# Ranking over 128 sums, picks of eight heads at a time on VectorE, and the one-hot gates of two pairs of tokens spread in one group

## The chip, the cores and the metric

One core of a Trainium2 chip runs the kernel. The metric is the device time of one execution in microseconds (us), and less is better. Engines are named as the profile names them: PE (TensorE; PEld is its weight loads), DVE (VectorE), ACT (ScalarE), POOL (GpSimd) and SP (SyncE, which issues the weight DMAs).

## The reference, cut to what matters

An encoder block over 256 tokens of width 2048, all float32: norm, projections, two kinds of attention, gates, an output projection, and then the part that this case is about, a product-key expert layer.

```python
q = (t @ w_pq).reshape(n_tok, 8, 2, 128)
sc = einsum('thcd,hckd->thck', q, sub_keys)          # (256, 8 heads, 2 halves, 128 keys)
top_s, top_i = lax.top_k(sc, 16)
cand_s = top_s[:, :, 0, :, None] + top_s[:, :, 1, None, :]      # 16 x 16 sums per head
cand_i = top_i[:, :, 0, :, None] * 128 + top_i[:, :, 1, None, :]
best_s, best_j = lax.top_k(cand_s, 16)
expert_idx = take_along_axis(cand_i, best_j)         # 8 heads x 16 experts of 16384
gate = softmax(best_s)
out[t] = sum over its 128 experts e of  gate * gelu(u[e] . t) * v[e]
```

## The kernel before, in words

**Chunks and bodies.** Every weight matrix goes through the core in chunks of 128 x 1024 floats (512 KB). Per chunk SP loads `raw` (four buffers), ACT rounds it into `hi` (L620, four buffers), DVE makes the rest `lo = raw - hi` (`lo_of`, L1000, two buffers), and PE multiplies `hi` by both halves of the activations (eight wide matmuls, "highs") and `lo` by the first half (eight narrow ones, "lows"). An even chunk goes highs, lows; an odd one lows, highs. So the order on PE is H0 L0 L1 H1 H2 L2 L3 H3. Four chunks are a body; slot `s` of body `it` is one chunk. On DVE slot `s` begins with `lo_of(s + 1)` and then holds other work, so a `lo` waits for what the slot before put on DVE's queue, and for the chunk two earlier to be done with its buffer. The order of work is written out by hand; each engine's queue is strictly in order.

**The expert layer.** 224 of the 256 tokens are computed densely: stage `u` (256 chunks, 64 bodies) makes gelu(u . t) for all 16384 experts, row block by row block of 128, into `act`; stage `down` (256 chunks, 64 bodies in two halves of 32) multiplies `act` by v. The last 32 tokens are computed from gathered rows: 64 gathers of `u_rows` by POOL (L574, buffers `rows0`, `rows1`), each followed by a dot product on DVE (`dot_of`, L1426), then 64 gathers of `w_down` rows, each added by DVE (`rows_at`, L1539 and L1542). `gather("u_rows", n)` waits for `dot_done >= n - 1`, `gather("w_down", n)` for `row_added >= n - 1`.

**Ranking.** In bodies 1 to 16 of stage `u` DVE ranks one head of one token half each (`best`): the 16 x 16 sums `cand` (L1338), the best 8 (L1341), replaced (L1344), indexed (L1348), the next 8 (L1351, L1354), then the two digits of the place (L1357 to L1361) and a one-hot comparison `pick` (L1364). POOL multiplies it by the key numbers (L563), and DVE sums it in the next body (`reduce_picks`, L1372). Body UR = 17 divides the softmax, PE turns gates and numbers after it, and body 18 copies them for the next stage.

**Spreading the gates.** From body U0 = 19 for 28 bodies, one pair of tokens per chunk: DVE makes `one_i` (`ones_of`, L1458, one buffer), POOL makes `one_j`, times the gate (L594, two instructions a pair, two buffers of a pair), PE multiplies them in full float32 ahead of the chunk (L1848, four recorded passes a pair), ACT copies the blocks still to come into `act` (L898), and DVE multiplies the blocks that are there (`gated_of`, L1467). DVE also multiplies `act` by each block's gelu (L1474). There is one dot per body at slot 3 (it follows the pair's work), and POOL's loop puts `gather("u_rows", k + 3)` ahead of pair 4k + 2. Bodies 47 to 63 hold no spreading and two dots each.

**Down.** The rows of each half are added at chunk 8 + 3.5 m of the half (`adds_of`). After each half PE's sums are kept as tiles. In the second half ACT squares eight tiles in slot 3 of bodies 33 and 34 (L959), and POOL, after `gather("w_down", 33)`, waits for both squares, folds them (three instructions of L607) and only then issues gather 34.

Body numbers of `down` go on to count from 0 at its first chunk.

Of the kernel before, what the change touches and what calls it, by code (L numbers as in the profile page):

```python
# [15 lines left out]
P = 128  # L16
# [72 lines left out]
UR = TT * PH + 1  # L89
# [33 lines left out]
DIVIDED = PH + 2  # L123
INDEXED = DIVIDED + 2

def dots_of(it, s):

    if it < UG:
        return (it - UR,) if s == 3 and it >= UR else ()
    return (UG - UR + 2 * (it - UG) + s // 2,) if s % 2 else ()  # L130


def adds_of(c):

    return tuple(m for m in range(PICKS) if 8 + m * 7 // 2 == c)
# [90 lines left out]
def build(nc, A, out):  # L226
    with ExitStack() as ctx:
# [47 lines left out]
        one_i = small("one_i", [P, 2, P])  # L275
        one_j = [small(f"one_j{i}", [P, 2, P]) for i in range(2)]
# [44 lines left out]
        cand = at("cand", ARENA + 104 * KB, [P, TOPK * TOPK])  # L321
        cand_b = at("cand_b", ARENA + 105 * KB, [P, TOPK * TOPK])
        pick = at("pick", ARENA + 106 * KB, [P, 2, TOPK, TOPK])
        pick_b = at("pick_b", ARENA + 96 * KB, [P, 2, TOPK, TOPK])
        best_s = at("best_s", ARENA + 108 * KB, [P, TOPK])
        best_j = at("best_j", ARENA + 108 * KB + 64, [P, TOPK], U32)
        half_u = at("half_u", ARENA + 108 * KB + 128, [P, 2, TOPK], U32)
        half_f = at("half_f", ARENA + 108 * KB + 256, [P, 2, TOPK])
        soft_sum = at("soft_sum", ARENA + 108 * KB + 448, [P, TT * PH])
# [69 lines left out]
        picked, picked_row = sem("picked"), sem("picked_row")  # L399
# [121 lines left out]
        def _(pool):  # L521
# [35 lines left out]
            kept = top_i[:].rearrange("p t h c k -> p (t h) c k")  # L557
            pool.wait_ge(top_kept, HC + 2)
            for first, row in ((0, PH), (PH, -PH)):
                with pool.Fori(first, first + PH) as it:  # L560
                    pool.wait_ge(picked, it + 2)
                    r = kept[:, bass.ds(it + row, 1), :, :].rearrange("p a c k -> p (a c) k").unsqueeze(2).to_broadcast([P, 2, TOPK, TOPK])
                    nc.gpsimd.tensor_tensor(pick_b[:], pick[:], r, ALU.mult).then_inc(picked_row, 1)  # L563

# [49 lines left out]
        def _(a):  # L614
# [244 lines left out]
            with a.Fori(1, DIVIDED - 1) as it:  # L859
                body("u", it, gelu_kept)  # L860
            body("u", DIVIDED - 1, gelu_and_exp)
            with a.Fori(DIVIDED, INDEXED) as it:
                body("u", it, gelu_kept)
            body("u", INDEXED, gelu_and_index)
            with a.Fori(INDEXED + 1, UR) as it:
                body("u", it, gelu_kept)

# [7 lines left out]
            body("u", UR, lambda it, s: (gelu_kept(it, s), exp_of(0, 2 * PH) if s == 1 else None))  # L875
# [9 lines left out]
            def gelu_split(j, e):  # L885
# [3 lines left out]
                if t < TD:  # L889
                    nc.scalar.activation(act[:, j, t:TD], upper[e][:, t:TD], ACT.Gelu)  # L890
                nc.scalar.activation(upper[e][:, 0:t], upper[e][:, 0:t], ACT.Gelu).then_inc(act_ready, 1)

            def keep_gates(it, s):
# [71 lines left out]
            down(0, 0, after=gelu_w)  # L965
            with a.Fori(1, HALF - 1) as it:
# [25 lines left out]
        def _(v):  # L992
# [331 lines left out]
            halves = top_s[:].rearrange("p t h c k -> p (t h) c k")  # L1324
            cut, cut2 = [P, TOPK, TOPK], [P, 2, TOPK, TOPK]

            def of_head(t, it):
                return t[:].rearrange("p t (h k) -> p (t h) k", k=TOPK)[:, bass.ds(it, 1), :].rearrange("p a k -> p (a k)")

            def best(body_it, s, row_of, before=None):  # L1330

                keep_u(body_it, s)
                it = row_of(body_it)
                if s == 0:
                    v.wait_ge(picked, body_it)
                    a = flat(halves[:, bass.ds(it, 1), 0, :]).unsqueeze(2).to_broadcast(cut)
                    b = flat(halves[:, bass.ds(it, 1), 1, :]).unsqueeze(1).to_broadcast(cut)
                    did(nc.vector.tensor_tensor(cand[:].rearrange("p (a b) -> p a b", a=TOPK), a, b, ALU.add))  # L1338
                    wait()
                    settle()  # L1340
                    did(nc.vector.max(best_s[:, 0:8], cand[:]))  # L1341
                    wait()
                    settle()
                    did(nc.vector.match_replace(cand_b[:], best_s[:, 0:8], cand[:], LOWEST))  # L1344
                if s == 1:
                    if before:
                        reduce_picks(body_it - 1, before(body_it - 1))
                    did(nc.vector.max_index(best_j[:, 0:8], best_s[:, 0:8], cand[:]))  # L1348
                    wait()
                    settle()  # L1350
                    did(nc.vector.max(best_s[:, 8:16], cand_b[:]))  # L1351
                    wait()
                    settle()
                    did(nc.vector.max_index(best_j[:, 8:16], best_s[:, 8:16], cand_b[:]))  # L1354
                if s == 2:
                    wait()
                    did(nc.vector.tensor_scalar(half_u[:, 0, :], best_j[:], 4, None, ALU.logical_shift_right))  # L1357
                    did(nc.vector.tensor_scalar(half_u[:, 1, :], best_j[:], 15, None, ALU.bitwise_and))
                    did(nc.vector.tensor_scalar(of_head(found_g, it), best_s[:], best_s[:, 0:1], None, ALU.subtract))
                    wait()  # L1360
                    did(nc.vector.tensor_copy(half_f[:], half_u[:]))  # L1361
                    wait()

                    nc.vector.tensor_tensor(pick[:], half_f[:].unsqueeze(3).to_broadcast(cut2),  # L1364
                                            iota16[:].unsqueeze(1).unsqueeze(1).to_broadcast(cut2), ALU.is_equal
                                            ).then_inc(picked, 1)

            def reduce_picks(done, row):

                v.wait_ge(picked_row, done)  # L1370
                ij = found_ij[:].rearrange("p c t (h k) -> p c (t h) k", k=TOPK)[:, :, bass.ds(row, 1), :]
                nc.vector.tensor_reduce(ij.rearrange("p c a k -> p c (a k)"), pick_b[:], AX.X, ALU.add).then_inc(best_ready, 1)  # L1372

            def row_1(body_it):
                return body_it + (PH - 1)

            def row_0(body_it):
                return body_it - (PH + 1)
            v.sem_inc(picked, 1)
# [4 lines left out]
            def divided(tt, step):  # L1384
                g = found_g[:, tt, :].rearrange("p (h k) -> p h k", k=TOPK)
                total = soft_sum[:, tt * PH:(tt + 1) * PH]
                if step == 0:
                    v.wait_ge(soft_ready, TT - tt)
                    did(nc.vector.tensor_reduce(total, g, AX.X, ALU.add))
                    wait()  # L1390
                    did(nc.vector.reciprocal(total, total))
                if step == 1:
                    wait()
                    return nc.vector.tensor_tensor(g, g, total.unsqueeze(2).to_broadcast([P, PH, TOPK]), ALU.mult)

            def best_and_divide(it, s):
                best(it, s, row_0, row_0)
                if s == 0:
                    divided(1, 0)
                if s == 1:  # L1400
                    did(divided(1, 1))
                if s == 2:
# [625 lines left out]
```

## Time and profile before

| | |
|---|---|
| time of the three runs | 2187.15 us median (2185.96 to 2187.82) |
| the profiled execution | 2187.54 us, its span 2185.8 us |
| busy share of the span | PE 97%, DVE 74%, ACT 51%, POOL 25% |
| mean granted PE clock | 0.991 |
| stage `u`, ranking bodies 1 to 16 | 794.0 to 975.9 us |
| first spreading body (19) | 996.7 to 1014.5 us |
| the other 27 spreading bodies | 1014.5 to 1341.7 us |
| bodies 48 to 63, nothing added | 1351.8 to 1512.7 us |

A body of plain chunks issues 64 matmuls, a spreading body 80. Positions are us from the span's start. In a timeline a row is a run of like instructions of one engine; in brackets behind it is the idle time of the engine ahead of it and what ended it. Consecutive DVE instructions overlap by some 0.08 us in their records.

### The profile page before, as it was taken

The page shows a single profiled execution, that of the slowest core. Times are in us where ns is not written, and L with a number is a line of the kernel's source. Part 1 is how long each engine was busy: PE and PEld are TensorE (multiplying, and loading weights), DVE is VectorE, ACT ScalarE, POOL GpSimd, SP SyncE. Part 2 cuts the span into 40 slices and gives each one's busy share as a digit, 9 for nine tenths or more (in the row PEclk, how much of TensorE's full clock was granted, in tenths as well). Part 3 has the DMA queues.
Part 4 walks back from the last instruction along what each step waited for, and adds up shares of the span by engine and source line. Part 5 has one row for each costly group of instructions (what it writes and reads, how often), then busy time and mean ns, then how long its engine had stood idle before and what let it go on. Part 6 is the DMA issues. An engine that isn't in the chain of part 4 may idle for free.

```text
span 2185.8 us, 41303 instructions
## 1 busy us (share of the span) xinstructions
PE 2128.4 (97%) x13474; PEld 1983.1 (91%) x13474; DVE 1609.3 (74%) x2656; ACT 1120.9 (51%) x1867; POOL 545.7 (25%) x403
## 2 busy tenths in 40 slices
PE   7999999999999999999999999999999999999997
PEld 6888888889988998888999999999999999899996
DVE  6555566667777889996777888887777776777776
ACT  5444455446454554555555555555555555555454
POOL 0000000000002001127999996332111110211110
PEclk9999999999999999999999999999999999999999
DMA  5655544445555555556666666898877776677773
GB/s 213 243 186 191 182 165 154 146 152 202 183 186 210 171 177 183 183 202 214 217 214 220 212 216 254 308 317 301 287 278 267 268 261 220 234 274 270 265 268 130
DMA packets 134460, 482.17 MB, mean 221 GB/s; under 512 B 15423, under 2 KB 18239, under 8 KB 134007
## 3 DMA queue, kind: packets, MB, share of 16 engines
q1 hardware_dynamic: 115958, 414.27, 54.2%
q0 software_dynamic: 18432, 67.12, 8.4%
q8 instruction: 26, 0.43, 0.1%
q14 instruction: 44, 0.35, 0.0%
HBM read 477.09 MB, written 4.24 MB: 220 GB/s over the span
## 4 chain that ended last, share of the span: by engine, by line
PE 55%; DVE 4%; issue 3%; ACT 1%; POOL 1%; DVEq 0%; ACTq 0%; POOLq 0%
PE ps L1861 19%; PE ps L1600 15%; PE ps L1865 10%; PE ps L1607 8%; PE ps L1848 3%; DVE lo L1000 1%; POOL one_j L594 1%; ACT hi L620 1%; DVE found_ij L1372 0%; DVE best_s L1351 0%; DVE best_j L1348 0%; DVE upper L1006 0%; DVE best_j L1354 0%; DVE x L1588 0%; PE ps L1917 0%
## 5 line engine op out<-in xcount | busy, mean ns | idle before, releaser
L1000 DVE TENSOR_TENSOR lo<-raw,hi 128x1024 fp32r<-128x1024 f32 x760 | 949.9, 1251 | 484.2 <-PE ps L1600 146.9
L620 ACT CAST hi<-raw 128x1024 fp32r<-128x1024 f32 x760 | 794.7, 1051 | 367.5 <-DMA raw<-w_down 143.0
L1600 PE MATMUL ps<-move_u,hi 128*128 128x448 f32 x2048 | 454.5, 370 | 0.0
L1861 PE MATMUL ps<-act_now,hi 128*128 128x448 f32 x2048 | 442.6, 367 | 0.4 <-issue 0.4
L1861 PEld LDWEIGHTS ps<-act_now,hi 128*128 128x128 f32 x2048 | 377.2, 189 | 26.8 <-issue 0.7
L1600 PEld LDWEIGHTS ps<-move_u,hi 128*128 128x128 f32 x2048 | 374.0, 190 | 24.7
L1600 PE MATMUL ps<-move,hi 128*128 128x512 f32 x1536 | 381.2, 397 | 10.7 <-ACT hi L620 10.0
L1600 PEld LDWEIGHTS ps<-move,hi 128*128 128x128 f32 x1536 | 282.6, 190 | 64.9 <-issue 9.9
L628 ACT COPY upper<-ps 128x224 f32<-128x224 f32 (+1 forms) x224 | 80.0, 357 | 485.6 <-PE ps L1600 485.3
L594 POOL TENSOR_SCALAR one_j<-iota,j_t,gate_t 128x128 f32<-128x128 f32 x224 | 295.7, 1326 | 10.6 <-PE ps L1848 8.9
L1607 PE MATMUL ps<-move_u,lo 128*128 128x224 f32 x2048 | 267.3, 278 | 14.7 <-DVE lo L1000 14.6
L1607 PEld LDWEIGHTS ps<-move_u,lo 128*128 128x128 f32 x2048 | 255.1, 192 | 21.6 <-DVE lo L1000 18.0
L1865 PEld LDWEIGHTS ps<-act_now,lo 128*128 128x128 f32 x2048 | 251.4, 192 | 9.3 <-issue 3.2
L1865 PE MATMUL ps<-act_now,lo 128*128 128x224 f32 x2048 | 252.7, 275 | 4.2 <-DVE lo L1000 4.2
L1607 PEld LDWEIGHTS ps<-move,lo 128*128 128x128 f32 x1536 | 198.7, 193 | 14.4 <-DVE lo L1000 4.2
L574 POOL DMA_INDIRECT rows<-w_down,idx x64 | 93.5, 1462 | 460.6 <-DVE acc L1542 423.1
L1607 PE MATMUL ps<-move,lo 128*128 128x256 f32 x1536 | 202.0, 285 | 5.2 <-DVE lo L1000 4.0
L574 POOL DMA_INDIRECT rows<-u_rows,idx x64 | 90.6, 1416 | 123.8 <-DVE dots L1426 110.8
L1507 DVE TENSOR_TENSOR act_now<-act,act_now 128x224 fp32r<-128x224 f32 x256 | 99.7, 390 | 14.3 <-ACT act_now L913 14.2
L1630 PE MATMUL ps<-move,hi 128*128 128x256 f32 x512 | 99.2, 291 | 3.7 <-DVE lo L1000 3.7
L527 POOL COPY q_now<-qk 128x256 f32 x8 | 4.1, 512 | 370.3 <-DVE qk L1013 213.8
L913 ACT CAST act_now<-act 128x224 fp32r (+1 forms) x256 | 95.3, 373 | 0.0
(194 smaller groups left out, 1710.0 us busy)
## 6 DMA issues: line engine op xcount, KB each, us to landing
raw<-w_u SPq DMA_DIRECT2D x256, 512.0 KB, 3.4
raw<-w_down SPq DMA_DIRECT2D x256, 512.0 KB, 3.5
raw<-w_qk SPq DMA_DIRECT2D x68, 512.0 KB, 3.3
raw<-w_gate SPq DMA_DIRECT2D x64, 512.0 KB, 3.3
raw<-w_out SPq DMA_DIRECT2D x32, 512.0 KB, 3.3
raw<-w_pq SPq DMA_DIRECT2D x32, 512.0 KB, 4.1
raw<-w_v SPq DMA_DIRECT2D x28, 512.0 KB, 3.3
raw<-w_o SPq DMA_DIRECT2D x24, 512.0 KB, 3.3
```

The costliest lines, as they stand in the source:

```text
L574: nc.gpsimd.indirect_dma_start(rows[n % 2][:], None, lines, bass.IndirectOffsetOnAxis(ap=idx[:, n:n + 1], axis=0)).then_inc(row_landed[n % ...
L594: ins = nc.gpsimd.tensor_scalar(one_j[n % 2][:, t % 2, :], iota128[:], j_t[:, t:t + 1], gate_t[:, t:t + 1], ALU.is_equal, ALU.mult)
L620: nc.scalar.copy(hi[slot][:], raw[slot][:]).then_inc(hi_ready, 1)
L628: nc.scalar.copy(upper[e][:, 0:w], ps[e][:, w:2 * w]).then_inc(upper_ready, 1)
L913: nc.scalar.copy(act_now[s % ACTS][:, 0:TD], pick1(act, j)).then_inc(act_hi_ready, 1)
L1000: nc.vector.tensor_tensor(lo[s % LOS][:], raw[s % RAW][:], hi[s % RAW][:].bitcast(F32), ALU.subtract).then_inc(lo_ready, 1)
L1507: nc.vector.tensor_tensor(act_now[s % ACTS][:, TD:2 * TD], pick1(act, j), act_now[s % ACTS][:, 0:TD].bitcast(F32), ALU.subtract).then_inc( ...
L1600: ins = nc.tensor.matmul(ps[bank][:, 0:2 * w], hi[slot][:, col:col + P], m, start=begins, stop=ends)
L1607: ins = nc.tensor.matmul(ps[bank][:, 0:w], lo[lslot][:, col:col + P], m[:, 0:w], start=False, stop=False, skip_group_check=True)
L1630: ins = nc.tensor.matmul(ps[bank][:, 0:T], w[:, col:col + P], x, start=begins, stop=ends)
L1861: return nc.tensor.matmul(ps[d][:, 0:2 * TD], hi[s % RAW][:, d * P:(d + 1) * P], act_now[s % ACTS][:], start=begins, stop=ends)
L1865: return nc.tensor.matmul(ps[d][:, 0:TD], lo[s % LOS][:, d * P:(d + 1) * P], act_now[s % ACTS][:, 0:TD], start=False, stop=False, skip_gro ...
```

## The change

Four things. **(1) Ranking:** of the 256 sums only 128 places are formed, 4 x 16 and 4 x 12 with 16 filled once; the ranking of a head is cut into the four slots, and its scores and places are kept. **(2) Picks:** digits, places and one-hot picks are made for all eight heads of a token half at a time, 1024 elements wide in two parts, all on DVE, by a table of slots (`PICK_AT`); POOL's multiply is gone. UR goes from 17 to 22, so everything behind it, spreading included, begins five bodies later, and bodies 1 to 21 are written out. **(3) Spreading:** pairs 2i and 2i + 1 are spread together, ahead of the even chunks alone, into one bank; `one_i` has two buffers, `one_j` four. **(4) Rows:** ten of the 64 dots move into bodies 0 to 4 of `down`; the adds of the first half come at chunk 28 + 2.75 m, those of the second at chunk 2 + 3.5 m.

```diff
-UR = TT * PH + 1
+UR = TT * PH + 6
 U0 = UR + 2
 J_KEPT = 2 * U0 - 1
...
+TOGETHER = 2
+def spread_at(n):
+    return SPREAD_BANKS[n // TOGETHER % SPREADS], n % TOGETHER * 2 * P
 def pairs_before(j):
-    return min(max(0, 2 * (j - J_KEPT) + 1), PAIRS)
+    return min(max(0, 2 * (j - J_KEPT)), PAIRS)
 def blocks_before(n):
-    return J_KEPT + (n + 1) // 2
+    return J_KEPT + n // 2 + 1
...
-DIVIDED = PH + 2
-INDEXED = DIVIDED + 2
+INDEXED = UR - 2
+PICK_AT = {1: {PH + 1: (0, 1, 2, 3), PH + 2: (4, 5, None, 6), PH + 3: (None, 7, None, 8), PH + 4: (None, None, None, 9),
+               PH + 5: (None, 10, None, 11), PH + 6: (None, None, None, 12), PH + 7: (None, 13, None, 14),
+               PH + 8: (None, None, None, 15), PH + 9: (None, 16, None, 17)},
+           0: {2 * PH + 1: (0, 1, 2, 3), 2 * PH + 2: (4, 5, 6, 7), 2 * PH + 3: (None, 8, 9, 10),
+               2 * PH + 4: (None, 11, 12, 13), 2 * PH + 5: (14, 15, 16, 17)}}
+SOFT_AT = {1: ((PH + 1, 0), (PH + 1, 2), (PH + 3, 0), (PH + 3, 2), (PH + 4, 0)),
+           0: ((2 * PH + 1, 0), (2 * PH + 1, 2), (2 * PH + 3, 0), (2 * PH + 4, 0), (2 * PH + 5, 0))}
+EXP_AT = {1: PH + 2, 0: 2 * PH + 2}
+WEIGHED = (STEPS - (UG - UR) - 2 * (CHUNKS["u"] // BODY - UG) + 1) // 2
 def dots_of(it, s):
     if it < UG:
         return (it - UR,) if s == 3 and it >= UR else ()
-    return (UG - UR + 2 * (it - UG) + s // 2,) if s % 2 else ()
-def adds_of(c):
-    return tuple(m for m in range(PICKS) if 8 + m * 7 // 2 == c)
+    n = UG - UR + 2 * (it - UG) + s // 2
+    return (n,) if s % 2 and n < STEPS else ()
+def adds_of(c, half):
+    first, apart = (2, 7 / 2) if half else ((WEIGHED + 2) * BODY, 11 / 4)
+    return tuple(m for m in range(PICKS) if first + int(m * apart) == c)
...
 # POOL: the multiply by top_i (L563) is gone; the loop over pairs
             for n in range(PAIRS):
                 if n % BODY == 2:
                     gather("u_rows", n // BODY + 3)
-                if n >= 2:
-                    pool.wait_ge(gates_spread, n - 1)
+                if n >= 2 * TOGETHER:
+                    pool.wait_ge(gates_spread, n - 2 * TOGETHER + 1)
                 for t in (2 * n, 2 * n + 1):
-                    ins = nc.gpsimd.tensor_scalar(one_j[n % 2][:, t % 2, :], iota128[:], j_t[:, t:t + 1], gate_t[:, t:t + 1],
+                    ins = nc.gpsimd.tensor_scalar(one_j[n % 4][:, t % 2, :], iota128[:], j_t[:, t:t + 1], gate_t[:, t:t + 1],
                                                   ALU.is_equal, ALU.mult)
...
 # DVE: ranking in four slots
+                if s == 0:
                     wait()
+                    did(nc.vector.tensor_tensor(cand[:, 0:4 * TOPK].rearrange("p (a b) -> p a b", b=TOPK),
+                                                s0[:, 0:4].unsqueeze(2).to_broadcast([P, 4, TOPK]),
+                                                s1.unsqueeze(1).to_broadcast([P, 4, TOPK]), ALU.add))
+                    did(nc.vector.tensor_tensor(cand[:, 4 * TOPK:8 * TOPK].rearrange("p (b a) -> p b a", b=4)[:, :, 4:TOPK],
...
+                keep_u(b, s)
+                wait()
+                if s == 0:
                     did(nc.vector.max(best_s[:, 0:8], cand[:]))
+                if s == 1:
+                    did(nc.vector.match_replace(cand_b[:], best_s[:, 0:8], cand[:], LOWEST))
+                    did(nc.vector.max_index(best_at[:, 0:8], best_s[:, 0:8], cand[:]))
+                if s == 2:
+                    did(nc.vector.max(best_s[:, 8:16], cand_b[:]))
+                if s == 3:
+                    did(nc.vector.max_index(best_at[:, 8:16], best_s[:, 8:16], cand_b[:]))
...
 # DVE: picks 6 to 17 are four times (compare, multiply, reduce) over [P, 4 heads, 16, 16]
+                found = [P, PH // 2 * TOPK, TOPK]
+                if n % 3 == 0:
+                    return did(nc.vector.tensor_tensor(pick[:].rearrange("p h k a -> p (h k) a"),
+                                                       at_ij[:, c, own].unsqueeze(2).to_broadcast(found),
+                                                       iota16[:].unsqueeze(1).to_broadcast(found), ALU.is_equal))
+                if n % 3 == 1:
+                    return did(nc.vector.tensor_tensor(pick[:], pick[:], top_i[:, tt, heads, c, :].unsqueeze(2)
+                                                       .to_broadcast([P, PH // 2, TOPK, TOPK]), ALU.mult))
+                return did(nc.vector.tensor_reduce(found_ij[:, c, tt, own], pick[:].rearrange("p h k a -> p (h k) a"), AX.X, ALU.add))
...
-            def ones_of(it, s):
-                n = it * BODY + s
-                if n:
-                    v.wait_ge(gates_spread, n)
+            def ones_of(n):
+                if n >= TOGETHER:
+                    v.wait_ge(gates_spread, n - TOGETHER + 1)
...
+            def spread_gates(it, s):
+                n = (it - U0) * BODY + s
+                if n + TOGETHER < PAIRS:
+                    ones_of(n + TOGETHER)
                 keep_u(it, s)
+                if n >= TOGETHER:
+                    gated_of(n - TOGETHER)
                 multiply_split(it, s)
                 dots_at(it, s)
...
 # PE: ahead of slots 0 and 2
+                    for m in range(s, s + TOGETHER):
+                        bank, col = spread_at(k * BODY + m)
+                        pe.wait_ge(one_i_ready, n + (m + 1))
+                        pe.wait_ge(one_j_ready, n + (m + 1))
+                        if not (isinstance(it, int) and it < U0 + 2):
+                            pe.wait_ge(gated, n + (m + 1 - 2 * BODY))
+                        for u in range(2):
+                            ins = nc.tensor.matmul(ps[bank][:, col + u * P:col + (u + 1) * P], one_i[m % 2][:, u, :],
+                                                   one_j[m % 4][:, u, :], start=True, stop=True)
+                        ins.then_inc(gates_spread, 1)
...
 # ACT: keep_gates waits for both pairs of its group; exp and the w_s gelu at their new bodies
+                a.wait_ge(gates_spread, n - n % TOGETHER + TOGETHER)
```

## Rows read from the trace of the kernel before

**Rows 1.** Windows: stretch and length, busy us (instructions) by engine, granted PE clock, DMA.

```profile
794.00:996.70 202.70, 188.14 (x1162) 176.06 (x1160) 182.53 (x369) 107.47 (x166) 37.95 (x21) 0.99 0.54 191
996.70:1014.50 17.80, 14.85 (x83) 14.19 (x83) 8.88 (x18) 6.57 (x13) 13.70 (x13) 0.81 0.55 187
1014.50:1341.70 327.20, 324.87 (x2162) 305.61 (x2161) 260.84 (x486) 173.65 (x378) 312.47 (x241) 1.00 0.64 217
1527.00:1820.00 293.00, 293.00 (x1867) 279.84 (x1867) 213.60 (x268) 153.66 (x233) 46.91 (x32) 1.00 0.76 273
1868.10:1884.00 15.90, 13.04 (x65) 12.11 (x65) 10.89 (x11) 5.72 (x9) 6.71 (x5) 0.79 0.55 199
```

**Rows 2.** Groups of DVE's instructions by shape, 600 to 1000 us.

```profile
L1364 DVE TENSOR_TENSOR pick<-half_f,iota 128x512 f32<-128x512 f32 x16 | 11.1, 693 | 0.6
```

**Rows 3.** Timeline of PEld in a middle spreading body, 1086 to 1099 us.

```profile
1086.44 0.61 PEld L1848 LDWEIGHTS ps<-one_j,one_i 128*128 128x128 f32 x4
1089.48 0.53 PEld L1848 LDWEIGHTS ps<-one_j,one_i 128*128 128x128 f32 x4
1089.93 0.97 PEld L1607 LDWEIGHTS ps<-move_u,lo 128*128 128x128 f32 x8
1092.76 0.52 PEld L1848 LDWEIGHTS ps<-one_j,one_i 128*128 128x128 f32 x4 [0.42 <-issue]
```

**Rows 4.** Timeline of DVE and POOL in that body, and of DVE in body 46.

```profile
1083.93 1.23 DVE L1000 TENSOR_TENSOR lo<-raw,hi 128x1024 fp32r<-128x1024 f32 x1 [1.14 <-PE ps L1607]
1085.79 1.22 DVE L1426 CUSTOM_DVE_ANT_0 rows<-rows,h_rows 128x1024 f32<-128x1024 f32 x1
1089.85 1.22 DVE L1000 TENSOR_TENSOR lo<-raw,hi 128x1024 fp32r<-128x1024 f32 x1 [0.80 <-PE ps L1607]
1089.96 1.78 POOL L594 TENSOR_SCALAR one_j<-iota,j_t,gate_t 128x128 f32<-128x128 f32 x1
1092.82 1.23 DVE L1000 TENSOR_TENSOR lo<-raw,hi 128x1024 fp32r<-128x1024 f32 x1 [1.01 <-PE ps L1600]
...
1326.99 1.23 DVE L1000 TENSOR_TENSOR lo<-raw,hi 128x1024 fp32r<-128x1024 f32 x1 [0.64 <-PE ps L1607]
1329.19 1.21 DVE L1426 CUSTOM_DVE_ANT_0 rows<-rows,h_rows 128x1024 f32<-128x1024 f32 x1
```

**Rows 5.** Timelines at two later bodies: a POOL instruction just ahead of a DVE one.

```profile
1250.90 0.80 POOL L594 TENSOR_SCALAR one_j<-iota,j_t,gate_t 128x128 f32<-128x128 f32 x1
1251.05 1.36 DVE L1000 TENSOR_TENSOR lo<-raw,hi 128x1024 fp32r<-128x1024 f32 x1 [0.81 <-PE ps L1600]
...
1263.25 1.84 POOL L594 TENSOR_SCALAR one_j<-iota,j_t,gate_t 128x128 f32<-128x128 f32 x1
1263.36 1.23 DVE L1000 TENSOR_TENSOR lo<-raw,hi 128x1024 fp32r<-128x1024 f32 x1 [0.77 <-PE ps L1600]
```

**Rows 6.** Timeline behind a dot in a body without spreading.

```profile
1385.95 1.23 DVE L1426 CUSTOM_DVE_ANT_0 rows<-rows,h_rows 128x1024 f32<-128x1024 f32 x1
1387.46 1.68 POOL L574 DMA_INDIRECT rows<-u_rows,idx  x1 [3.09 <-DVE dots L1426]
```

**Rows 7.** Timeline and a window at two waits of PE, and the start of spreading.

```profile
905.27 1.15 PE L1607 MATMUL ps<-move_u,lo 128*128 128x224 f32 x8 [1.94 <-DVE lo L1000]
906.70:909.90 3.20, 3.20 (x10) 2.85 (x9) 3.17 (x5) 0.84 (x3) 1.28 (x1) 0.50 0.34 132
996.47 4.58 POOL L594 TENSOR_SCALAR one_j<-iota,j_t,gate_t 128x128 f32<-128x128 f32 x4
```

**Rows 8.** Timeline of the fold in `down`, and gather 34's issue to landing.

```profile
1866.18 6.02 POOL L607 TENSOR_TENSOR sq<-sq 128x1024 f32<-128x1024 f32 x3 [56.72 <-ACT sq L959]
1866.82 3.43 DVE L1542 SCALAR_TENSOR_TENSOR acc<-rows,w_s,acc 128x1024 f32<-128x1024 f32 x1
1873.41 0.72 PEld L1865 LDWEIGHTS ps<-act_now,lo 128*128 128x128 f32 x3 [3.01 <-issue]
...
DMA to landing us min/median/max: 5.5/5.5/5.5
```

More of the change, by code:

```diff
@@ L964, in kept_tiles @@
                         ins.then_inc(x2_scaled, 1)
-            down(0, 0, after=gelu_w)
-            with a.Fori(1, HALF - 1) as it:
+            down(0, 0)
+            with a.Fori(1, WEIGHED) as it:
+                down(it, 0)
+            down(WEIGHED, 0, after=gelu_w)
+            with a.Fori(WEIGHED + 1, HALF - 1) as it:
                 down(it, 0)
@@ L1322, in keep_u, with rank @@
                     sum_of("u", it * 2, 0, upper[0][:, 0:TD], TD)
[L1324 to L1333, printed above, removed]
+            def rank(b, s):
+                tt, h = (1, b - 1) if b <= PH else (0, b - PH - 1)
+                own = slice(h * TOPK, (h + 1) * TOPK)
+                s0, s1 = top_s[:, tt, h, 0, :], top_s[:, tt, h, 1, :]
+                best_s, best_at = found_g[:, tt, own], best_j[:, tt, own]
@@ L1343, in best @@
[L1343 to L1348, printed above, removed]
-                    wait()
[L1350 to L1354, printed above, removed]
@@ new lines, in softmax_of @@
+            def softmax_of(tt, step):
+                g = found_g[:, tt, :].rearrange("p (h k) -> p h k", k=TOPK)
+                total = soft_sum[:, tt, :]
+                over = [P, PH, TOPK]
+                wait()
+                if step == 0:
+                    did(nc.vector.tensor_copy(first_s[:], g[:, :, 0]))
+                if step == 1:
+                    nc.vector.tensor_tensor(g, g, first_s[:].unsqueeze(2).to_broadcast(over), ALU.subtract).then_inc(best_ready, 1)
+                if step == 2:
+                    v.wait_ge(soft_ready, TT - tt)
+                    did(nc.vector.tensor_reduce(total, g, AX.X, ALU.add))
+                if step == 3:
+                    did(nc.vector.reciprocal(total, total))
+                if step == 4:
+                    did(nc.vector.tensor_tensor(g, g, total.unsqueeze(2).to_broadcast(over), ALU.mult))
@@ new lines, in experts_of @@
+            def experts_of(b, s):
+                if b <= 2 * PH:
+                    rank(b, s)
+                else:
+                    keep_u(b, s)
+                for tt in (1, 0):
+                    for step in range(5):
+                        if SOFT_AT[tt][step] == (b, s):
+                            softmax_of(tt, step)
+                    n = PICK_AT[tt].get(b, (None,) * BODY)[s]
+                    if n is not None:
+                        pick_of(tt, n)
+                if (b, s) == PAIR_AT[0]:
+                    wait()
+                    did(nc.vector.scalar_tensor_tensor(out=e_pair[:, 0, :], in0=found_ij[:, 1, 1, :], scalar=float(NK),
+                                                       in1=found_ij[:, 0, 1, :], op0=ALU.mult, op1=ALU.add))
+                if (b, s) == PAIR_AT[1]:
+                    wait()
+                    nc.vector.tensor_scalar(e_pair[:, 1, :], e_pair[:, 0, :], float(NK * NK), None, ALU.add).then_inc(e_ready, 1)
```

221 lines of the change are left out of this document (90 added, 131 removed).

## The prediction

> **What bounds the kernel now.** I read the page first: PE is the busiest engine by far, so in most stages the time is PE's own and only its waits can be won or added. Then windows by stage. Plain chunks cost PE 293.0 us for 1867 matmuls, which is 10.04 us for the 64 of a body, and there it never waits. Against that, the 18 bodies from 794.0 to 996.7 us take 202.7, the first spreading body 17.8 at a granted clock of 0.81, the other 27 spreading bodies 327.2 (12.12 each), and one body of `down` 15.9 at a clock of 0.79 [rows 1]. Everything the change can do lies in those four excesses: 202.7 - 18 x 10.04 = 22.0, then the first spreading body, then the 27, then 15.9 - 10.04 = 5.9. In all of them I then read the timeline, to see which engine PE waits for last.
>
> In a spreading body (positions from its first spread, T = 1086.44) PE spreads a pair at T, at T + 3.04 and at T + 6.32, the last one 0.42 late; without that wait it is at T + 5.90, so an undisturbed body is 2 x 5.90 = 11.80. A pair's passes take 0.45 (1089.48 to 1089.93) [rows 3]. What was late is POOL: in the window of the 27 bodies it is busy 312 of 327 us [rows 1]. It is that slow because of DVE: a `one_j` instruction takes 0.8 us alone, but 1.78 when it starts at 1089.96, just behind a DVE `lo` (1089.85 to 1091.07): it ends 0.67 after the `lo` does [rows 4]. One that starts 0.15 ahead of a `lo` still goes through in 0.80, one that starts 0.11 ahead takes 1.84 [rows 5]. So a POOL instruction that begins inside a `lo`, or under some 0.13 ahead of it, is held to the `lo`'s end and ends 0.65 after it.
>
> **Ranking and picks.** A DVE instruction over 512 elements takes 0.69 [rows 2], one over 1024 takes 1.22 [rows 4], so 0.16 plus 1.04 per 1024: 0.29 for 128, 0.4 for 224. Half a plain body is 5.02. With two `lo` (2.45), one sum (0.4), the two candidate instructions (0.4), one max (0.3) and a replace and an index with their loads (0.7), slots 0 and 1 come to 4.3; before, the same work over 256 elements, the second max and index and POOL's sum stood there, and that was the excess. A pick adds 1.22: 5.5 in bodies 11, 13 and 15, which is 0.5 over each. Slots 2 and 3 with a pick are 4.7 and fit. In bodies 18 to 20 halves with two picks are 5.3 (0.3 over, three times); body 21 has four picks, 10.9 in all, 0.9 over. I add 1.2 for body 1, which still starts behind the last key ranking, 0.5 for each of the two exponentials (their table loads delay ACT's `hi`), and 1.4 for the turns of gates and numbers, which PE now pays without a wait to hide one in. Sum 1.2 + 1.5 + 1.0 + 1.8 + 1.4 = 6.9; no wait for `found_ready` (it is set a body earlier). Gain 22.0 - 6.9 = **-15.1**. If all picks hid it would be -19; if each of the 24 wide picks showed half its 1.22, -2 or so.
>
> **The start of spreading.** POOL's first four `one_j` took 996.47 to 1001.05 [rows 7]. Before, PE needed two of them; the first group needs four, so PE waits 2 x 0.78 longer: **+1.5**. POOL's queue there holds nothing else than gather 3, which was behind them anyway.
>
> **The other 27 bodies.** This is the part that decides. With four buffers POOL may run two groups ahead, but its queue is in order, and gather k + 3 stands ahead of pair 4k + 2. That gather waits for `dot_done >= k + 2`, so for the dot of slot 3 of the body before the one that uses pair 4k + 2. POOL gets to it early, waits there, and then has to make the gather and four instructions (pairs 4k + 2 and 4k + 3) before PE's second group. Before, it had only two to make, and PE could take the last pair one chunk later. Step by step, from T:
>
> - Both pairs are now ahead of the even chunk, so even chunks end 0.44 later, odd ones as before. DVE's `lo` of slots 1 and 3 (before at T + 3.41 and at T - 2.51) move to T + 3.85 and T - 2.07; that of slot 2 stays at T + 6.38, which is 0.5 behind PE's second spread point.
> - The dot begins 1.86 after the slot 3 `lo` (1083.93 to 1085.79) and ends at T + 0.57 [rows 4]. After: T + 1.01. Its distance grows, as `act` fills, to 2.20 in the last spreading body [rows 4], so the end runs from about T + 0.92 to T + 1.35.
> - Behind a dot the next `lo` follows at once, and a gather that waited for the dot starts 0.28 after its end and takes 1.68 [rows 6]. It ends at T + 2.97.
> - First `one_j`: T + 3.01 to 3.79. The second would start at 3.79, only 0.06 ahead of the `lo` at 3.85: held, it ends at 5.07 + 0.65 = 5.72. Third: 6.50. The fourth starts inside the `lo` of T + 6.38 to 7.61 and ends at 8.27. PE starts 0.23 after it, at T + 8.50, which is 2.60 late: a body of **14.40**. In the earliest bodies the second starts 0.15 ahead and passes; then the third is held (5.72), the fourth ends at 6.51, PE is 0.84 late: a body of 12.64. By the drift that should be some four bodies, and 23 are of the long kind.
> - Then PE's clock. Where the matmuls stood 1.94 us idle (905.27), the granted clock is 0.50 from 906.7 to 909.9 [rows 7]; where they waited 3.01, the body lost 5.9, so 2.85 beyond the wait itself [rows 1, 8]. The 2.3 us gap of a long body lies between. I take the lesser, 3.2 us at half speed, 1.6 us: **16.0** a body. Bounds: none (14.4) and 2.85 (17.25).
>
> 4 x 12.64 + 23 x 16.0 = 418.6, against 327.2: **+91.4**.
>
> The Trainium skill bears on the lock. "SBUF — State Buffer", section "Who interferes with whom", says that a DVE instruction with two SBUF inputs contends only with GpSimd's reads, that one side is then fully blocked for the other's whole instruction, and that descriptor generation is inferred not to be touched by such an instruction. By the first half the trace agrees (1.78 against 0.80); by the last, a gather behind a dot would not be stretched by the `lo` beside it and would end sooner, the second instruction would pass, and the sum would be that of rival B, 2199. I go by the measured 1.68.
>
> **Rows of the last 32 tokens.** The dots moved into `down` meet plain bodies whose DVE has room; the same two a body were hidden in bodies 48 to 63, where PE never waited. I cost them and the denser adds (a row every 6.9 us, against 5.5 to land) at nothing, up to 2 if landings run late.
>
> The second half's adds are another matter. Add 2 of that half comes at chunk 2 + 7 = 9, slot 1 of body 34; before it was chunk 15. Its row is gather 34, which POOL issues only behind the fold, and the fold waits for ACT's square in slot 3 of body 34. DVE therefore stands in slot 1 for something that slot 3 starts, and the `lo` for chunk 3 of the body is behind it. Nothing deadlocks, since ACT runs a chunk or two ahead. In time: the fold started at 1866.18 and took 6.02, with a DVE add of 3.43 in its way, which is 1.28 of work; with DVE idle I take 4.1, so 1870.3; the gather 0.3 later, 5.5 to land: 1876.1; add, rest and `lo`, 2.8: 1878.9 [rows 8]. PE would take that `lo` at about 1865.3 (before, it took its lows there without a wait): 13.6 late. The clock goes to half as it did before, 2.85 more. Against the 5.9 that the fold cost before, which falls away: 13.6 + 2.85 - 5.9 = **+10.6**. If the fold is as slow as before, 12.5; if the row lands sooner by 1, 9.6.
>
> **Sum.** Profiled execution 2187.5 (span 2185.8 and 1.7 around it; 0.4 over the median, no more than the runs' spread): 2187.5 - 15.1 + 1.5 + 91.4 + 10.6 = **2276**.
>
> **The rivals.** *A: the long bodies, but the clock stays up.* Against it: both waits above were followed by half clock, the one of 1.94 too; for it: ranking's excess of 1.2 a body was not, and a wait can fall well or badly for the clock. 4 x 12.64 + 23 x 14.40 = 381.8, +54.6: 2239. *B: the second `one_j` passes each time.* It stands 0.06 from the edge, and my positions are good to 0.1 or so; against it is the drift of the dot's end by 0.4. 27 x 12.64 = 341.3, +14.1: 2199. *C: the clock loses more, 2.85 a body.* +120: 2305. *D, the other side: POOL keeps pace.* If the gather found its dot done, deeper buffers would hide all of POOL and the body would be 11.80: 318.6, -8.6, so 2187.5 - 15.1 + 1.5 - 8.6 + 10.6 = 2176. It decides at a last `one_j` by T + 5.67; four of them and the gather from the dot's end need 0.28 + 1.68 + 0.04 + 4 x 0.78 = 5.1 even unheld, so the dot would have to end by T + 0.5, and not be held once. In its favour is only that the two engines' order could settle otherwise than I read it. *E: the row of add 2 does not stop DVE:* 16 less in any case; B with E would be 2182.
>
> **How the numbers follow.** Main case 0.42, A 0.21, B 0.14, C 0.10, D 0.10, something else 0.03. The likeliest gives 2276; its own range is 2262 to 2290, by the number of long bodies (18 to 27) and the ranking's bounds. For 8 in 10 the range reaches from B to C, 2197 to 2305. 0.2% (4.4 us) is about what a measurement of this kernel can tell. Faster by more: D and B with E, 0.12; within: 0.03; slower: 0.85.
>
> **What would show it.** Ranking bodies of 10.04 with little PE idle; `found_ij` on DVE at 1.22 each. In the spreading stage POOL idle ahead of gathers on DVE's dots (none before), gathers of 1.68, `one_j` at 1.8 twice a body, PE waiting on `one_j` ahead of every second chunk alone, and a granted clock near 0.85. In `down`, one wait of DVE for gather 34 of over 12 us. The prediction is wrong in its main term if PE's waits ahead of L1848 are under 1 us, in the clock if they are 2.3 and the clock reads 0.99, and in the last if no `rows` wait shows at body 34.

## The result and the profile after

The changed kernel takes 2226.93 us (median of four runs, 2223.38 to 2231.48), against 2187.49 before: 1.018 times as long, interval 1.016 to 1.020, or 39.4 us slower. The forecast was 88.5 slower. Its profiled run took 2223.38 (span 2221.6), the lowest of the four, so the trace explains 35.8 us of the 39.4. Two of the four runs are 7 to 8 us longer; they have no trace, and what they lost is open.

First the page of after: busy shares, and the chain that ended last.

```profile
PE 2125.2 (96%) x13474; PEld 1982.0 (89%) x13474; DVE 1581.3 (71%) x2612; ACT 1112.0 (50%) x1863; POOL 456.1 (21%) x387
...
PE 83%; POOL 8%; DVE 4%; issue 4%; DMA 1%; ACT 0%; DVEq 0%; SPq 0%; ACTq 0%; POOLq 0%
...
L607 POOL TENSOR_SCALAR one_j<-iota,j_t,gate_t 128x128 f32<-128x128 f32 x224 | 225.4, 1014 | 1.2
```

POOL has less work than before (21% against 25%) and still holds 8% of the chain. That points to something that POOL waits for, and not to the amount of its work. Then the windows of after, for the same stretches as [rows 1]: the 23 ranking bodies, the first spreading body, the other 27, and the slow body of `down`.

```profile
793.70:1027.30 233.60, 232.51 (x1482) 221.30 (x1480) 186.50 (x367) 130.27 (x203) 4.87 (x5) 1.00 0.65 211
1027.30:1045.80 18.50, 14.85 (x83) 13.90 (x83) 8.73 (x16) 6.19 (x13) 12.66 (x13) 0.82 0.53 173
1045.80:1418.30 372.50, 329.87 (x2162) 310.70 (x2161) 262.81 (x485) 167.40 (x379) 261.36 (x240) 0.99 0.54 190
1891.00:1915.50 24.50, 12.54 (x64) 11.65 (x63) 8.99 (x12) 6.00 (x10) 9.28 (x7) 0.72 0.42 146
```

Ranking: 233.6 less 23 plain bodies of 10.04 leaves 2.7, where it was 22.0: -19.3. First spreading body: +0.7. The 27: 372.5 against 327.2, +45.3. Body of `down`: 24.5 against 15.9, +8.6. Together +35.3, and the spans differ by 35.8. The last columns say something else: the 27 bodies ran at a granted clock of 0.99, not near 0.85.

The waits in the window of the 27 bodies:

```profile
POOL rows L587 <- DVE dots L1451: 109.8, 27, 6.4
...
PE ps L1877 <- POOL one_j L607: 39.1, 25, 1.8
```

POOL stands ahead of all 27 gathers, 4.1 us each; PE then waits for `one_j`. One middle body (T = 1096.65), DVE, POOL, PEld and PE:

```profile
1096.45 1.22 DVE L1451 CUSTOM_DVE_ANT_0 rows<-rows,h_rows 128x1024 f32<-128x1024 f32 x1
1097.59 1.22 DVE L1018 TENSOR_TENSOR lo<-raw,hi 128x1024 fp32r<-128x1024 f32 x1
1100.51 1.23 DVE L1018 TENSOR_TENSOR lo<-raw,hi 128x1024 fp32r<-128x1024 f32 x1 [0.77 <-PE ps L1631]
1103.04 1.23 DVE L1018 TENSOR_TENSOR lo<-raw,hi 128x1024 fp32r<-128x1024 f32 x1 [0.58 <-PE ps L1624]
...
1097.95 1.77 POOL L587 DMA_INDIRECT rows<-u_rows,idx  x1 [3.79 <-DVE dots L1451]
1099.75 8.27 POOL L607 TENSOR_SCALAR one_j<-iota,j_t,gate_t 128x128 f32<-128x128 f32 x8
...
1102.64 0.55 PEld L1877 LDWEIGHTS ps<-one_j,one_i 128*128 128x128 f32 x4
1105.15 0.52 PEld L1877 LDWEIGHTS ps<-one_j,one_i 128*128 128x128 f32 x4 [1.97 <-issue]
...
1105.16 0.71 PE L1877 MATMUL ps<-one_j,one_i 128*128 128x128 f32 x4 [1.78 <-POOL one_j L607]
```

The dot's two records end at 1097.67; the gather starts 0.28 later and ends at T + 3.07; the fourth `one_j` ends at 1104.92, which is T + 8.27, and PE has the second pair at T + 8.50. All of this is the forecast's chain. What it left out is the row at 1102.64: the first pair of the group is ready at T + 6, and PE spreads it then and waits for the second alone. (In the first POOL row eight `one_j` are merged; the first four are the group's, 1099.75 to 1104.92, the second and the fourth held to 1.86 and 1.74. The other four belong to the next group.)

### The profile page after: what moved, and what is told of

The parts are those of the page before. It is cut to its first block, busy times and chain, and to the rows that moved or that the text cites. A ratio compares the mean times of both kernels' runs of the same rounds, so it can differ in the third digit from the quotient of the medians.

```text
span 2221.6 us, 40823 instructions
## 1 busy us (share of the span) xinstructions
PE 2125.2 (96%) x13474; PEld 1982.0 (89%) x13474; DVE 1581.3 (71%) x2612; ACT 1112.0 (50%) x1863; POOL 456.1 (21%) x387
## 4 chain that ended last, share of the span: by engine, by line
PE 83%; POOL 8%; DVE 4%; issue 4%; DMA 1%; ACT 0%; DVEq 0%; SPq 0%; ACTq 0%; POOLq 0%
PE ps L1624 28%; PE ps L1893 19%; PE ps L1631 15%; PE ps L1897 10%; PE ps L1654 7%; POOL one_j L607 6%; POOL rows L587 2%; DVE lo L1018 1%; PE ps L1877 1%; PE ps L1730 1%; PE ps L1748 1%; DVE rows L1451 1%; DVE one_i L1477 0%; DVE act L1487 0%; PE ps L1739 0%
## 5 line engine op out<-in xcount | busy, mean ns | idle before, releaser
L1018 DVE TENSOR_TENSOR lo<-raw,hi 128x1024 fp32r<-128x1024 f32 x760 | 937.5, 1234 | 554.5 <-PE ps L1631 208.1
L1897 PEld LDWEIGHTS ps<-act_now,lo 128*128 128x128 f32 x2048 | 251.4, 192 | 19.3 <-issue 12.3
L1631 PEld LDWEIGHTS ps<-move_u,lo 128*128 128x128 f32 x2048 | 250.0, 192 | 5.3 <-DVE lo L1018 1.5
L1631 PE MATMUL ps<-move_u,lo 128*128 128x224 f32 x2048 | 250.1, 275 | 1.2 <-DVE lo L1018 1.1
L607 POOL TENSOR_SCALAR one_j<-iota,j_t,gate_t 128x128 f32<-128x128 f32 x224 | 225.4, 1014 | 1.2
L587 POOL DMA_INDIRECT rows<-u_rows,idx x64 | 106.0, 1656 | 524.9 <-ACT gates_s L870 290.1
L1631 PEld LDWEIGHTS ps<-move,lo 128*128 128x128 f32 x1536 | 197.9, 192 | 14.6 <-DVE lo L1018 4.3
L1877 PE MATMUL ps<-one_j,one_i 128*128 128x128 f32 x448 | 67.6, 284 | 46.3 <-POOL one_j L607 42.7
L1877 PEld LDWEIGHTS ps<-one_j,one_i 128*128 128x128 f32 x448 | 60.4, 193 | 54.7 <-issue 47.9
```

Source lines behind the costliest of these rows:

```text
L587: nc.gpsimd.indirect_dma_start(rows[n % 2][:], None, lines, bass.IndirectOffsetOnAxis(ap=idx[:, n:n + 1], axis=0)).then_inc(row_landed[n % ...
L607: ins = nc.gpsimd.tensor_scalar(one_j[n % 4][:, t % 2, :], iota128[:], j_t[:, t:t + 1], gate_t[:, t:t + 1], ALU.is_equal, ALU.mult)
L1018: nc.vector.tensor_tensor(lo[s % LOS][:], raw[s % RAW][:], hi[s % RAW][:].bitcast(F32), ALU.subtract).then_inc(lo_ready, 1)
L1631: ins = nc.tensor.matmul(ps[bank][:, 0:w], lo[lslot][:, col:col + P], m[:, 0:w], start=False, stop=False, skip_group_check=True)
L1877: ins = nc.tensor.matmul(ps[bank][:, col + u * P:col + (u + 1) * P], one_i[m % 2][:, u, :], one_j[m % 4][:, u, :], start=True, stop=True)
L1897: return nc.tensor.matmul(ps[d][:, 0:TD], lo[s % LOS][:, d * P:(d + 1) * P], act_now[s % ACTS][:, 0:TD], start=False, stop=False, skip_gro ...
```

## The experiments

All are edits of the changed kernel; the difference to before is with each. Before ran beside them at 2185.94 (experiments 1 to 4) and 2187.50 (5 to 8). The changed kernel was not run again; differences to it use its 2226.93, measured beside a before of 2187.49, so they can be off by one or two us. Waits, body lengths and single times that no row here shows are read from the traces of the same runs.

**1. The gather behind the pairs.** Gather k + 3 goes ahead of pair 4k + 4 in place of pair 4k + 2.

```diff
-                if n % BODY == 2:
-                    gather("u_rows", n // BODY + 3)
+                if n % BODY == 0 and n:
+                    gather("u_rows", n // BODY + 2)
...
-            for n in range(PAIRS // BODY + 3, STEPS):
+            for n in range(PAIRS // BODY + 2, STEPS):
```

> The changed kernel, but POOL's gather k + 3 stands ahead of pair 4k + 4 instead of pair 4k + 2, so that the group ahead of chunk 2 no longer has it in front. Queue theory (the gather's wait for DVE's dot, with four one_j instructions behind it, makes PE late ahead of every chunk 2): the 27 spreading bodies go from 372.5 us to 27 x 11.8 to 11.9 = 319 to 321, PE's waits ahead of L1877 disappear after the first body, and the time falls by 51 to 54 to about 2171. Group theory (eight passes in a row, the pairwise buffers, or ACT's copies cost it): the bodies stay at 13.9 and the time within 3 us of 2227.

Measured: 2173.82 (2170.04 to 2175.88), 0.994 of before (0.992 to 0.995). The window of its 27 bodies:

```profile
1048.00:1367.70 319.70, 319.70 (x2162) 307.09 (x2161) 269.02 (x485) 169.51 (x378) 300.81 (x236) 1.00 0.65 222
```

Each body is 11.84 and PE has no gap in 319.7 us. POOL is busy 301 of 320, a larger share than in the kernel after, and PE never waits for it. It still waits for a dot at times, ahead of 5 gathers and 7.2 us in all, against 27 and 109.8. Moving one line of queue order takes back 52.8 of 372.5: with the pairs grouped, the place of the gather is the whole loss of this stage.

**2. Pairs one at a time**, as before the change, with the gather left where it was.

```diff
-TOGETHER = 2
+TOGETHER = 1
...
-                        if not (isinstance(it, int) and it < U0 + 2):
-                            pe.wait_ge(gated, n + (m + 1 - 2 * BODY))
+                        if not (isinstance(it, int) and it == U0):
+                            pe.wait_ge(gated, n + (m + 1 - SPREADS))
```

> The changed kernel with one pair ahead of each chunk again (TOGETHER = 1; POOL waits for the pair two back), ranking, picks, dots and adds as changed. Both theories: the 27 spreading bodies return to 12.1 each, 327 us, so about 45 less, 2178 to 2182. It tells how much of the result lies outside the spreading: with the row wait in down left in, the rest should stand at -19 (ranking and picks) and +8.6 (down) against the kernel before. If ranking was not the gain, it will be above 2187.

Measured: 2177.39 (2175.47 to 2179.14), 0.996 (0.994 to 0.997). Bodies of 12.0 to 12.3 first and 11.84 towards the end, where before had 12.12 on the mean. Here the mean is 12.05 (325.3 for the 27), some 0.2 over the 11.84 of experiment 1, where the kernel after loses 2.05 (13.89). `TOGETHER` also sets how far POOL runs ahead, now two pairs in place of four, and its waits show what that does: it waits for no dot at all, since it comes to the gather late enough to find it done. In a middle body of this run the dot ends at 1095.61 and the gather starts at 1097.50, behind a `one_j`, and takes 1.03. What is left of the loss goes with POOL's load, as in the kernel before (busy 304 of 318 us). Gather and grouping are bad only together. Which part of grouping it takes, PE's need of two pairs at once or POOL's running ahead into the wait, this edit can't separate.

**3. PE waits for both pairs first.** The step that the forecast had assumed, made true.

```diff
-                        pe.wait_ge(one_i_ready, n + (m + 1))
-                        pe.wait_ge(one_j_ready, n + (m + 1))
+                        pe.wait_ge(one_i_ready, n + (s + TOGETHER))
+                        pe.wait_ge(one_j_ready, n + (s + TOGETHER))
```

> The changed kernel, but PE waits for both pairs of a group before it spreads either. Per-pair theory (what kept the long bodies at 13.88 rather than 14.40 is that PE spreads pair 4k + 2 while it waits for pair 4k + 3): long bodies become 14.3 to 14.4, PE's gap 2.2 to 2.3 us instead of 1.8, and the granted clock falls in many more of them (each costing about 1.6). Without any drop +11 us; with a drop in every long body +49, 2276. Rival (the long bodies are short of 14.40 because DVE's or POOL's steps are shorter than read): no change, 2227.

Measured: 2247.93 (2245.64 to 2252.26), 1.028 (1.026 to 1.030), 21.0 over the changed kernel. Its 27 bodies, and two neighbours among them by window; then PE's rows in these two.

```profile
1049.50:1443.40 393.90, 339.32 (x2161) 315.84 (x2161) 265.68 (x485) 170.04 (x378) 260.63 (x240) 0.97 0.51 180
1115.50:1129.80 14.30, 12.07 (x82) 11.27 (x81) 9.38 (x19) 6.48 (x14) 10.00 (x9) 1.00 0.51 182
1129.80:1145.70 15.90, 13.68 (x82) 12.64 (x82) 9.45 (x19) 6.34 (x14) 9.98 (x9) 0.89 0.47 165
```

```profile
1123.62 1.15 PE L1877 MATMUL ps<-one_j,one_i 128*128 128x128 f32 x8 [2.23 <-POOL one_j L607]
...
1137.94 1.29 PE L1877 MATMUL ps<-one_j,one_i 128*128 128x128 f32 x8 [2.23 <-POOL one_j L607]
1138.88 3.34 PE L1624 MATMUL ps<-move_u,hi 128*128 128x448 f32 x8
```

Four short bodies (12.80 to 12.96), 15 long ones of 14.34 and eight of 15.9. Both numbers of the forecast for a long body (14.40, and 16.0 with the clock) are there. The gap is 2.23 in both rows; behind the first eight highs take 1.86, behind the second 3.34, at half the clock. So a gap of this length is followed by the lower clock in 8 of 23 bodies, not in all. The eight aren't strewn at random: each comes two or three bodies behind the last, never in the next one. In each the granted clock falls to 0.50 only 0.8 to 1.5 us after PE has begun again.

**4. The dot first in its slot**, ahead of the gates and the multiply.

```diff
+                dots_at(it, s)
                 if n >= TOGETHER:
                     gated_of(n - TOGETHER)
                 multiply_split(it, s)
-                dots_at(it, s)
```

> The changed kernel, but in slot 3 of a spreading body DVE does the dot ahead of gated_of and the multiply, so that it ends 0.5 (early bodies) to 0.9 us (late ones) sooner. Queue theory with the edge (the second one_j instruction behind the gather just misses its start ahead of DVE's next lo): every body becomes one of the short kind, 12.4 to 12.5, so 27 x 12.45 = 336 against 372.5, the time 35 less, about 2190. If there is no edge and the loss is only the chain's length: 0.5 to 0.9 a body, 13 to 24 less. Group theory: no change.

Measured: 2178.77 (2178.67 to 2179.06), 0.997 (0.995 to 0.998). The first of the 27 bodies takes 12.38, the next 14 take 11.84, the others 11.84 to 12.4. None of the expectations gave this: 35 less was the best of them, and 48 came. DVE and POOL in a middle body:

```profile
1118.65 1.22 DVE L1451 CUSTOM_DVE_ANT_0 rows<-rows,h_rows 128x1024 f32<-128x1024 f32 x1
1120.20 1.22 DVE L1018 TENSOR_TENSOR lo<-raw,hi 128x1024 fp32r<-128x1024 f32 x1
...
1120.15 1.04 POOL L587 DMA_INDIRECT rows<-u_rows,idx  x1 [2.93 <-DVE dots L1451]
1121.23 3.82 POOL L607 TENSOR_SCALAR one_j<-iota,j_t,gate_t 128x128 f32<-128x128 f32 x4
```

The gates and the multiply, which stood ahead of the dot, now stand between it and the `lo`. The gather starts 0.05 ahead of the `lo` instead of 0.36 inside it, and takes 1.04 instead of 1.77. The dot begins 1.48 after its slot's `lo` instead of 1.86. The four `one_j` behind it take 3.82 in place of 5.17 (1099.75 to 1104.92 in the kernel after), since the second now ends ahead of the next `lo`. Two savings of 0.4 and 0.7 us and this one of 1.35 so move a body from 13.89 to 11.84: the edge is steep, since a POOL instruction that starts just inside a `lo` is held for nearly all of it. POOL still stands ahead of all 27 gathers, 76.8 us in all, and PE waits for `one_j` 1.7 us in the stage. So it isn't the standing that costs, but what is left to do between the dot and PE's need.

**5. Gathers 34 and 35 ahead of the fold.**

```diff
-            for n in range(PICKS + 2):
+            for n in range(PICKS + 4):
...
-            for n in range(PICKS + 2, STEPS):
+            for n in range(PICKS + 4, STEPS):
```

> The changed kernel, but POOL issues gathers 34 and 35 of w_down ahead of its wait for ACT's squares and of the fold. Row theory (DVE stands at add 2 in slot 1 of body 34 for a gather that is queued behind the fold): the body of 24.5 us in down becomes 10 to 12, the time falls by 12.5 to 14.5, to about 2213. Fold theory (the body is long because POOL's fold holds DVE off the shared port, as in the kernel before, and the clock falls): it stays above 15, and no more than 9 us are gained.

Measured: 2211.28 (2209.41 to 2215.88), 1.012 (1.010 to 1.013) of before and 15.6 under the changed kernel. The add of row 34, its gather and the fold in this kernel's timeline; then the body's window:

```profile
1888.58 1.28 DVE L1564 SCALAR_TENSOR_TENSOR acc<-rows,w_s,acc 128x1024 f32<-128x1024 f32 x1
...
1873.03 1.00 POOL L587 DMA_INDIRECT rows<-w_down,idx  x1 [44.36 <-DVE acc L1561]
1893.60 6.55 POOL L620 TENSOR_TENSOR sq<-sq 128x1024 f32<-128x1024 f32 x3 [11.54 <-ACT sq L974]
```

```profile
1894.90:1905.90 11.00, 10.66 (x65) 9.66 (x64) 9.84 (x9) 5.17 (x8) 8.16 (x5) 1.00 0.59 195
```

The gather is issued 15.5 us ahead of its add, which stands in no wait, and the body falls from 24.5 to 11.0, the clock at 1.00. The fold takes 6.55, but no row waits for it. The 15.6 is 1 to 3 us more than expected; this kernel's profiled run also has one drop of the clock among its spreading bodies where that of the changed kernel has two.

**6. The second half's adds from chunk 8**, so behind the squares as they were.

```diff
-    first, apart = (2, 7 / 2) if half else ((WEIGHED + 2) * BODY, 11 / 4)
+    first, apart = (8, 7 / 2) if half else ((WEIGHED + 2) * BODY, 11 / 4)
```

> The changed kernel with the second half's adds at chunk 8 + 3.5 m as before. Row theory: add 2 is again behind gather 34 in time, the body in down returns to 15.9 us (the fold's own cost with a fall of the clock), so 8.6 less, about 2218. If the down difference has another source (the moved dots, the denser adds of the first half): no change there.

Measured: 2215.60 (2213.06 to 2218.01), 1.013 (1.011 to 1.014), 11.3 under the changed kernel. The slow body is 14.6 at a granted clock of 0.88 (15.9 was expected), and what is left of it is the fold on POOL against DVE's `lo` and add:

```profile
1897.52 6.30 POOL L620 TENSOR_TENSOR sq<-sq 128x1024 f32<-128x1024 f32 x3 [63.64 <-ACT sq L974]
1897.67 3.33 DVE L1018 TENSOR_TENSOR lo<-raw,hi 128x1024 fp32r<-128x1024 f32 x1 [0.98 <-PE ps L1897]
1900.92 2.31 DVE L1564 SCALAR_TENSOR_TENSOR acc<-rows,w_s,acc 128x1024 f32<-128x1024 f32 x1
```

**7. Ranking and picks without the grouping**: edits 2 and 6 together.

> Ranking, picks, the five bodies' shift and the moved dots alone: pairs spread one by one and the second half's adds at chunk 8, both as before. What ranking and picks are worth: 22.0 - 2.7 = 19.3 us by the trace of the changed kernel, so 2168 here if the dots in down and the first half's denser adds cost nothing; 2172.4 if my recorded 15.1 was right.

Measured: 2170.19 (2165.76 to 2171.14), 0.992 (0.990 to 0.993). Ranking, picks and the moved dots without the grouping are worth 17.3 us, where 19.3 was expected if the dots and the denser adds cost nothing; it does not separate these parts. The slow body of `down` is still 14.7 here, and four others of that stage are 0.2 to 0.8 longer than 10.04, 1.7 us in all; why wasn't looked into.

**8. Both mends**: edits 1 and 5 together, grouping kept.

> Both mends of the changed kernel: gather k + 3 behind pair 4k + 3, and gathers 34 and 35 ahead of the fold. If the two losses are separate they add: g1's 2173 less 12.5 to 14.5, 2159 to 2161, a ratio of 0.987 to the kernel before.

Measured: 2162.42 (2161.04 to 2162.84), 0.989 (0.987 to 0.990): the fastest version, 25.1 us under before and 64.5 under the changed kernel. Its windows, as those of after above:

```profile
795.60:1029.30 233.70, 232.59 (x1483) 221.43 (x1481) 186.59 (x367) 130.41 (x203) 4.88 (x5) 1.00 0.68 211
1029.30:1047.60 18.30, 14.66 (x82) 13.74 (x83) 8.77 (x16) 6.17 (x12) 17.46 (x17) 0.81 0.53 174
1047.60:1367.30 319.70, 319.70 (x2161) 307.15 (x2161) 268.36 (x485) 169.53 (x378) 303.41 (x236) 1.00 0.67 222
1845.90:1857.40 11.50, 10.28 (x65) 9.65 (x65) 9.94 (x10) 4.40 (x7) 6.75 (x5) 1.00 0.69 228
```

Against before: -19.2, +0.5, -7.5, -4.4. The sum is -30.6 and the difference of the spans 26.5; the rest lies in a ranking stage that begins 1.6 later and in six bodies of `down` that are 0.2 to 0.6 longer, 2.0 in all.

## Why the prediction was right in direction and wrong in size

**The step that failed** is one of the long body: "The 2.3 us gap of a long body lies between. I take the lesser, 3.2 us at half speed, 1.6 us: 16.0 a body." It was charged to all 23 long bodies, 36.8 us. In the trace two of the 23 have it (15.5 us; granted clock 0.50 in the row below, the 1.2 GHz level), 3.2 us in all.

```profile
1190.00:1193.40 3.40, 3.40 (x16) 3.22 (x15) 0.17 (x1) 0.82 (x1) 1.34 (x2) 0.50 0.14 58
```

The size of the drop was right (1.6), its frequency wasn't: I took what followed one gap of 1.94 us and one of 3.01 as what always follows a gap of 2.3, though rival A named the ranking bodies whose waits had left the clock alone. With the gap that I had forecast (experiment 3: 2.23) it is 8 of 23; with the real one (1.78) it is 2 of 23. The same 1.78 stands in the long bodies of experiments 5 and 6, whose spreading is unchanged: 1 of 23 and 2 of 24 there, so 5 of 70 in all. The share grows between these two lengths. Which gaps are followed by the lower clock stays open; the regular distances in experiment 3 speak for the moment at which a gap falls and against mere chance, but no run sets that moment.

**The gap itself** was 1.78, because PE's waits are per pair. The forecast let the first pair of the second group wait for the second one; it is spread meanwhile, and 0.44 of passes come off. A long body is 13.89, not 14.40: 23 x 0.51 = 11.7 us. Experiment 3 shows that this is the cause, since waiting for both gives 14.34. (33.6 for the clock and 11.7 for the gap are 45.3 of the term's error of 46.1: 91.4 forecast, 45.3 measured, which is the same number by accident.) The short bodies (12.36 to 12.54) give the rest. The other three terms were too dear as well, by 4.2, 0.8 and 2.0, so no error made up for another.

**Right in that term:** 4 short and 23 long bodies, as forecast, one of the short ones not at the start but just behind a body at half clock; a fourth `one_j` at T + 8.27 to the hundredth, which is better than the steps were (the gather ended 0.10 late, and the second `one_j` began 0.04 inside the `lo` and not 0.06 ahead of it); the gather as the cause of it (experiment 1, which also gives rival D's body, 11.84 for its 11.80, and nearly its time, 2173.8 for 2176); and the two `one_j` held by a `lo` in each body. Rival A (2239) is nearest to the measured time: it has no clock loss, and 14.40 for each long body.

**Ranking and picks**: -19.3 against -15.1. Body 1 lost 1.36 (1.2 forecast), the two turns 0.67 each (1.4 in all). The halves that are 0.3 to 0.9 too long (1.5 and 1.8) and the exponentials (1.0) lost nothing: DVE falls behind in one half and catches up in the next, and two `lo` buffers cover that. DVE in bodies 11 and 12 runs without a gap from one pick over the next, and then waits for PE again:

```profile
904.66 1.22 DVE L1399 TENSOR_REDUCE found_ij<-pick 128x64 f32<-128x1024 f32 x1
905.80 1.22 DVE L1018 TENSOR_TENSOR lo<-raw,hi 128x1024 fp32r<-128x1024 f32 x1
...
908.09 1.23 DVE L1018 TENSOR_TENSOR lo<-raw,hi 128x1024 fp32r<-128x1024 f32 x1
...
910.60 1.22 DVE L1018 TENSOR_TENSOR lo<-raw,hi 128x1024 fp32r<-128x1024 f32 x1 [0.75 <-PE ps L1624]
```

**The start of spreading**: +0.7 for +1.5, by the same per-pair wait: PE waits 3.30 for the first pair and 0.36 more for the second, against 2.95 before. In experiment 3, where it waits for both, it is one wait of 4.8. The clock of 0.82 was there before as well.

**Rows in `down`**: +8.6 for +10.6, and the mechanism is the one forecast. DVE, POOL and PE of the kernel after:

```profile
1901.94 1.28 DVE L1564 SCALAR_TENSOR_TENSOR acc<-rows,w_s,acc 128x1024 f32<-128x1024 f32 x1 [12.78 <-DMA rows<-w_down,idx]
...
1892.80 4.49 POOL L620 TENSOR_TENSOR sq<-sq 128x1024 f32<-128x1024 f32 x3 [63.58 <-ACT sq L974]
1897.55 0.96 POOL L587 DMA_INDIRECT rows<-w_down,idx  x1 [0.27 <-POOL sq L620]
...
1904.80 2.02 PE L1897 MATMUL ps<-act_now,lo 128*128 128x224 f32 x8 [11.96 <-DVE lo L1018]
```

DVE stands in slot 1 for a row whose gather is behind a fold that slot 3 starts. The fold took 4.5 (4.1 forecast, 6.02 before, when DVE worked beside it). The add began 4.4 after its gather, which I had at 5.5, and PE waited 12.0 for 13.6. Rival E (the row doesn't stop DVE) is refuted. The ten dots moved into `down` cost at most 0.4 here, a body of 10.4.

**Two small sums** on record don't come out. 5.9 less the wait of 3.01 is 2.89 and not 2.85, which would make rival C 2306. And if each of the 24 wide picks showed half of its 1.22, the gain in ranking would still be near 4 (22.0 - 3.6 - 14.6) and not 2. Neither moves the 2276.

**The range** held, since it was built from the rivals and not from the likeliest alone.

## What to carry to other kernels

An in-order queue makes an operation that waits a gate for all behind it: ask of each gather or DMA what it waits for, and put it behind the compute that the critical engine needs next. Deeper buffers don't help where the queue itself stands still (argued from POOL's 109.8 us of waits with four buffers; no run changed the buffers alone). Standing there is free as long as the work between the end of the wait and the critical engine's need is short enough (experiment 4). Consuming several items at once moves the need for the last of them earlier by a whole item; where the waits are per item, the early ones still hide work, and a forecast must read at which grain the consumer waits. A clock drop seen behind one or two gaps is no price for all: count how often such gaps are followed by one before charging it to every body.

## What the runs showed of the hardware

A gather is held by DVE as a compute instruction is: 1.77 us when it starts 0.36 inside a `lo`, 1.04 when it starts 0.05 ahead of one, 0.96 with DVE idle. The Trainium skill, "SBUF — State Buffer", section "Who interferes with whom", infers that descriptor generation isn't touched by a DVE instruction with two SBUF inputs. These rows don't decide that: the gather also reads its `idx` from SBUF on POOL, and by the same section a `lo` holds an instruction of GpSimd that reads SBUF. That a start 0.05 ahead is enough to pass says only that what is held stands at the gather's beginning. The reverse holds too: three 128x1024 instructions on POOL took 4.49 with DVE idle and 6.30 beside it, and then a `lo` of DVE took 3.33 in place of 1.23. Equal gaps of PE (2.23) were followed by either clock level.
